# First phase of a streaming encoder step: weight tiles ahead of token rows, normalised rows in two buffers, scale and shift on ScalarE

## The chip, the core and the metric

One Trainium2 chip, one core of it. The time is device microseconds of one execution of the whole step, the median of three runs; lower is better. TensorE runs the matmuls and transposes (PE in the profile, PEld its weight loads), VectorE is DVE, ScalarE is ACT, GpSimd is POOL, and SyncE (SP) issues most of the loads. Each engine runs its own instruction list in the order in which it is written and meets the others only through semaphores.

## The reference, cut to what matters

The step is a two-layer encoder over 512 prompt tokens and 32 sample tokens, 2048 features wide. Only its beginning is touched here:

```python
xp = _layer_norm(x_prompt, ln_in_g, ln_in_b)      # (512, 2048)
xs = _layer_norm(x_sample, ln_in_g, ln_in_b)      # (32, 2048)
for l in range(DEPTH):                            # 2 layers
    fq, fk, ..., gate = _in_proj(xp, w_in[l])     # z = x @ W_in
    mk, mv = _mem_kv(mem_prompt, w_mem_kv[l])     # 256 memory tokens @ (2048, 1024)
    outs = (_fox_prompt(...), _band_prompt(...), _band_prompt(...), _cross(mq, mk, mv))
    xp = _merge(xp, outs, gate, w_out[l], ln_g[l], ln_b[l])
    ...                                           # the same for xs, with caches
def _layer_norm(x, g, b):
    mu = jnp.mean(xf, -1, keepdims=True)
    var = jnp.mean(jnp.square(xf - mu), -1, keepdims=True)
    return (xf - mu) * lax.rsqrt(var + LN_EPS) * g + b
```

## The kernel before, in words

**Split products.** A weight tile is 128 output columns of a matrix, held as `WR` [128, 2 slots, 16 chunks, 128]. Every matmul operand is split into a rounded high part and the rest: ScalarE casts `WR` to `WH` (`w_hi`, line 1012), VectorE subtracts to get `WL` (`w_lo`, line 1549), and TensorE runs three passes of 16 chunks per tile: WH by high input, WL by high input, WH by low input. The passes wait on `hi` and `lo`. A tile with 256 memory columns is 48 matmuls (`mem_tile`, line 952). Even tiles use slot 0, odd tiles slot 1; a new tile is loaded into a slot once `w_lo` of the tile two before is done (`load_first`, `load_weights`), is cast once the matmuls of that tile are done (`zd`), and can be multiplied once its result has been copied out of PSUM (`zf`, `MT` copy in `mem_done`).

**The first phase** (0 to 82.5 us) is layer 0's eight memory tiles, called tile 0 to 7 here, and beside them the first layer norm. The token rows come as five tiles of rows (`XT` four times 128 tokens, `XTS` 32 tokens; queue order in `sync`). Each gets a row sum (`first_sum`: tile 0 on ScalarE, the others on VectorE), a mean (`first_mean`), a sum of squared differences on ScalarE (`first_square`), then one shared reciprocal root (`first_rstd`, with `first_seed` on ScalarE) and the normalisation in place (`first_norm`, line 2131). TensorE transposes the rows chunk by chunk into three rotating PSUM banks (`turn_x`, line 934: four transposes per 128 features; the sample rows in one go ahead of chunk 0, line 928). VectorE applies scale and shift per feature into `OY` (`first_affine`, line 2149), ScalarE casts to `XH` (`first_hi`, line 1447) and issues the output of two chunks at a time, and VectorE subtracts to get `XL` (`x_lo`, line 2090). The sample columns have their own steps (`first_sample`, `first_sample_low`).

**What sets the order.** The lists `PE_PLAN`, `ACT_PLAN`, `DVE_PLAN` give for layer 0 the order of these steps on each engine, by name and number: ("w", 3) on VectorE is `w_lo` of tile 5, since `w_lo` of tile 0 stands before the list and ("w1", 0) is tile 1; ("mem", j) on ScalarE is `mem_done(0, j)`, the copy out of tile j and the cast of tile j + 2; ("x", g) is a pair of chunks. `TURNED` says after which third matmul of which memory tile TensorE turns which chunk. After the eight tiles TensorE runs `forget` (lines 899 and 906; the first needs all of `XH`, the second `XL` by pairs), then the first head's projections (line 579).

**Buffers.** `XT` lies over `XL`, so no part of `XL` is written until the last transpose is done: in the plan all ("low", g) stand behind ("x", 7).

Of the kernel before, what the change touches and what calls it, by code (L numbers as in the profile page):

```python
# [88 lines left out]
TURNED = {5: {2: 0, 4: 1, 7: 2, 9: 3, 12: 4, 14: 5}, 6: {2: 6, 4: 7, 7: 8, 9: 9, 12: 10, 14: 11},  # L89
          7: {1: 12, 3: 13, 5: 14, 7: 15}}  # L90
ACT_PLAN = [
    [("w1", 0), ("sum", 0), ("square", 0), ("mem", 0), ("square", 1), ("square", 2), ("mem", 1), ("square", 3),
     ("square", 4), ("seed", 0), ("mem", 2), ("mem", 3), ("mem", 4), ("sample", 0), ("x", 0), ("x", 1), ("x", 2),
     ("mem", 5), ("x", 3), ("x", 4), ("x", 5), ("mem", 6), ("x", 6), ("x", 7), ("mem", 7)],
# [3 lines left out]
    [("w1", 0), ("sum", 1), ("sum", 2), ("w", 0), ("sum", 3), ("sum", 4), ("w", 1), ("rstd", 0), ("norm", 0),  # L98
     ("w", 2), ("norm", 1), ("norm", 2), ("norm", 3), ("norm", 4), ("w", 3), ("sample", 0), ("x", 0), ("x", 1),
     ("w", 4), ("x", 2), ("mv", 4), ("x", 3), ("w", 5), ("x", 4), ("x", 5), ("mv", 5), ("x", 6), ("x", 7),   # L100
     ("low", 0), ("low", 1), ("low", 2), ("low", 3), ("low", 4), ("mv", 6), ("low", 5), ("low", 6), ("low", 7),
     ("mv", 7), ("w", 6), ("w", 7), ("tokens", 0)],
# [2438 lines left out]
```

## Time and profile before

| | us |
|---|---|
| median of 3 runs (lowest, highest) | 1881.48 (1880.87, 1881.88) |
| the profiled execution, its own time | 1881.82 |
| its span | 1879.9 |
| first head's projections start at | 82.53 |
| PE busy over the span | 1842.5 |

Start times are counted from the start of the span; the profiled execution's time is 1.9 us longer than its span. In a timeline row the first number is the start, the second the length, "x16" the instructions merged into the row, and the bracket says how long the engine stood idle just before and whose result ended that. The first phase is some 4% of the span and ends where TensorE leaves `forget`; the rest of the program isn't edited.

### The profile page before, as it was taken

Reading aid. Unit: us, or ns where it says so; the run is one execution under the profiler, and the core shown is the slowest. Engines: PE = TensorE matmul, PEld = TensorE weight load, DVE = VectorE, ACT = ScalarE, POOL = GpSimd, SP = SyncE. Lnnn points to the kernel's source line nnn. Section 1 sums busy time; section 2 is a strip of 40 time slices with the busy share of each in tenths; the row PEclk is TensorE's granted clock in tenths of the full one; section 3 lists DMA queues with packets and bytes.
Section 4 is the critical chain, followed back from the end, with each engine's and each line's share of the span. In section 5 each row is a group of like instructions: output and inputs, shape, how many; then the busy total and the mean of one; then the engine's idle time right before and its main releaser. Section 6 shows DMA issues by size and latency. Waiting matters only on the chain.

```text
span 1879.9 us, 36203 instructions
## 1 busy us (share of the span) xinstructions
PE 1842.5 (98%) x14704; PEld 1819.0 (97%) x14704; DVE 1481.5 (79%) x2085; ACT 971.9 (52%) x1583; POOL 161.3 (9%) x285
## 2 busy tenths in 40 slices
PE   7999999999999999999999999999999999999996
PEld 6999999999999999999999999999999999999996
DVE  6978877777798896777887687777788888767776
ACT  6455455444545456544574555555554555554444
POOL 0011110000000101000001111000000010100000
PEclk9999999999999999999999999999999999999998
DMA  8623333333323335655664233332333233535563
GB/s 300 235 82 125 123 125 127 115 126 105 114 104 108 112 122 186 222 205 206 217 229 152 83 123 117 119 113 99 107 110 107 96 121 106 201 137 201 198 218 133
DMA packets 71647, 273.83 MB, mean 146 GB/s; under 512 B 10136, under 2 KB 20000, under 8 KB 59184
## 3 DMA queue, kind: packets, MB, share of 16 engines
q1 hardware_dynamic: 44144, 202.12, 31.0%
q0 software_dynamic: 16928, 55.44, 8.5%
q10 hardware_dynamic: 10432, 14.29, 2.1%
q8 instruction: 98, 1.61, 0.3%
q14 instruction: 45, 0.37, 0.1%
HBM read 238.94 MB, written 35.50 MB: 146 GB/s over the span
## 4 chain that ended last, share of the span: by engine, by line
PE 87%; DVE 4%; ACT 4%; issue 2%; DMA 2%; SPq 0%; ACTq 0%; DVEq 0%
PE GB L725 46%; PE GB L637 18%; PE GB L579 8%; PE GB L952 3%; PE AB L666 3%; PE AB L708 3%; DMA WR<-in_wt 2%; PE AB L677 2%; PE GB L594 1%; ACT WH L1096 1%; ACT WH L1012 1%; DVE WL L1549 1%; DVE WL L1686 0%; PE AB L713 0%; ACT S L1026 0%
## 5 line engine op out<-in xcount | busy, mean ns | idle before, releaser
L1096 ACT CAST WH<-WR 128x1024 fp32r<-128x1024 f32 x322 | 335.9, 1048 | 403.9 <-PE GB L725 158.6
L1686 DVE TENSOR_TENSOR WL<-WR,WH 128x1024 fp32r<-128x1024 f32 x322 | 393.5, 1227 | 115.8 <-ACT WH L1096 111.6
L725 PE MATMUL GB<-XH,WH 128*128 128x272 f32 x1472 | 426.3, 290 | 2.5 <-DVE WL L1686 2.5
L725 PE MATMUL GB<-TLOW,WH 128*128 128x272 f32 x1472 | 423.8, 288 | 0.0
L725 PE MATMUL GB<-XH,WL 128*128 128x272 f32 x1472 | 423.3, 288 | 0.0
L725 PE MATMUL GB<-XL,WH 128*128 128x272 f32 x1472 | 421.1, 290 | 0.0
L725 PEld LDWEIGHTS GB<-XH,WH 128*128 128x128 f32 x1472 | 277.4, 188 | 3.4 <-DVE WL L1686 2.9
L1012 ACT CAST WH<-WR 128x2048 fp32r<-128x2048 f32 x92 | 175.6, 1908 | 198.8 <-PE GB L637 154.7
L725 PEld LDWEIGHTS GB<-XH,WL 128*128 128x128 f32 x1472 | 277.6, 189 | 0.0
L725 PEld LDWEIGHTS GB<-TLOW,WH 128*128 128x128 f32 x1472 | 276.8, 188 | 0.0
L725 PEld LDWEIGHTS GB<-XL,WH 128*128 128x128 f32 x1472 | 274.2, 188 | 0.4
L1549 DVE TENSOR_TENSOR WL<-WR,WH 128x2048 fp32r<-128x2048 f32 x92 | 210.7, 2291 | 56.6 <-ACT WH L1012 56.2
L725 PE MATMUL GB<-TX,WH 128*128 128x272 f32 x736 | 216.0, 293 | 0.0
L725 PE MATMUL GB<-TX,WL 128*128 128x272 f32 x736 | 212.3, 289 | 0.0
L637 PE MATMUL GB<-XL,WH 128*128 128x272 f32 x960 | 141.3, 288 | 0.0
L637 PE MATMUL GB<-XH,WH 128*128 128x272 f32 x960 | 140.1, 288 | 0.3 <-ACT WH L1012 0.3
L637 PE MATMUL GB<-XH,WL 128*128 128x272 f32 x960 | 140.0, 288 | 0.1
L725 PEld LDWEIGHTS GB<-TX,WH 128*128 128x128 f32 x736 | 138.4, 188 | 0.9
L725 PEld LDWEIGHTS GB<-TX,WL 128*128 128x128 f32 x736 | 138.8, 189 | 0.0
L637 PEld LDWEIGHTS GB<-XL,WH 128*128 128x128 f32 x960 | 128.4, 188 | 0.3
L637 PEld LDWEIGHTS GB<-XH,WH 128*128 128x128 f32 x960 | 127.8, 188 | 0.5 <-issue 0.5
L637 PEld LDWEIGHTS GB<-XH,WL 128*128 128x128 f32 x960 | 127.9, 188 | 0.3 <-DVE WL L1549 0.3
(281 smaller groups left out, 2906.4 us busy)
## 6 DMA issues: line engine op xcount, KB each, us to landing
WR<-in_wt SPq DMA_DIRECT2D x92, 1024.0 KB, 4.8
WR<-in_wt SPq DMA_DIRECT2D x184, 512.0 KB, 4.2
XR<-out POOLq DMA_DIRECT2D x64, 136.0 KB, 2.7
out<-OY ACTq DMA_DIRECT2D x24, 272.0 KB, 2.2
o_rest<-BD POOLq DMA_DIRECT2D x20, 272.0 KB, 5.1
out<-OY ACTq DMA_DIRECT2D x8, 544.0 KB, 6.0
out<-KT POOLq DMA_DIRECT2D x16, 272.0 KB, 2.4
out<-VT POOLq DMA_DIRECT2D x16, 272.0 KB, 2.4
```

Of the source, the lines that this page charges most:

```text
L579: mm = pe.matmul(GB[:, 2 * s + hf, 0:HALF], w[:, s, k, :], x[:, k, hf * HALF:(hf + 1) * HALF], start=(k == 0 and i == 0), stop=(k == KC - ...
L594: mm = pe.matmul(GB[:, 2 * s, 0:HALF], w[:, s, k, :], x[:, k, half(0)], start=(first and k == 0), stop=(last and k == KC - 1))
L637: mm = pe.matmul(GB[:, 2 * s + hf, 0:HALF], w[:, s, k, :], x[:, k, half(hf)], start=(at == 0), stop=(at == 3 * KC - 1))
L666: mm = pe.matmul(AB[0:r, b, at:at + w], q[:, t0:t0 + r], k, start=(p == 0), stop=(p == 2))
L677: mm = pe.transpose(AB[:, j // 4, P * (j % 4):P * (j % 4 + 1)], S[:, at:at + P], ident[:, :])
L708: mm = pe.matmul(AB[:, 3, P * i:P * (i + 1)], V[:, kb, :], pt_col(j), start=(b == 0), stop=(b == len(g.blocks[i]) - 1))
L725: mm = pe.matmul(out, w[:, k, :], x[:, k, :], start=(k == 0 and i == 0), stop=(k == KS - 1 and i == 2))
L952: mm = pe.matmul(GB[:, 2 * s, 0:NMEM], w[:, s, k, :], x[:, k, :], start=(at == 0), stop=(at == 3 * KC - 1))
L1012: act.copy(WH[:, s, :, :], WR[:, s, :, :]).then_inc(hi, 1)
L1096: act.copy(weight_block(p, name)[0], weight_source(name)).then_inc(b_hi, 1)
L1549: dve.tensor_tensor(WL[:, s, :, :], WR[:, s, :, :], WH[:, s, :, :].bitcast(F32), ALU.subtract).then_inc(lo, 1)
L1686: dve.tensor_tensor(lo_part, weight_source(name), hi_part.bitcast(F32), ALU.subtract).then_inc(b_lo, 1)
```

## The change

Six things change, all in layer 0's first phase.

1. **Load order (SP).** Weight tile 1 goes ahead of token rows 0, tile 2 (still behind `w_lo` of tile 0) ahead of rows 1, tile 3 (behind `w_lo` of tile 1) ahead of rows 3, tile 4 ahead of the three small transposition constants, and tile 5 ahead of the other constants.
2. **Row sum 2** moves from VectorE to ScalarE (`ACT_SUMS`), with a semaphore of its own, `x_sum_a`.
3. **Scale and shift** of the chunks (`first_affine`) moves to ScalarE, the cast to `XH` (`first_hi`) to VectorE. ScalarE now waits for its own result and for `x_smp` before it issues each output.
4. **Token rows** 0 and 1 lie over `TX` (`XTA`), rows 2 and 3 over the lower half of `XL` (`XTB`), so `XL`'s upper half is free from the start and ("low", 0) to ("low", 3) stand among the chunks.
5. **Transposes** are no longer in tiles 5, 6 and 7 (6, 6 and 4 chunks) but in tiles 6 and 7, eight each.
6. **In `mem_done`** of layer 0 the copy out of PSUM stands ahead of the cast of the next weight tile, and the plans of ScalarE and VectorE are written anew.

```diff
-TURNED = {5: {2: 0, 4: 1, 7: 2, 9: 3, 12: 4, 14: 5}, 6: {2: 6, 4: 7, 7: 8, 9: 9, 12: 10, 14: 11},
-          7: {1: 12, 3: 13, 5: 14, 7: 15}}
+TURNED = {6: {1: 0, 2: 1, 4: 2, 6: 3, 8: 4, 10: 5, 12: 6, 14: 7},
+          7: {0: 8, 2: 9, 4: 10, 6: 11, 8: 12, 10: 13, 12: 14, 14: 15}}
+ACT_SUMS = (0, 2)
...
-        XT = sb_at("XT", [P, NT - 1, DM], top[0])
+        XTB = sb_at("XTB", [P, 2, DM], top[0] + 4 * KS * TOK)
...
+        XTA = sb_at("XTA", [P, 2, DM], top[0])
         TX = sb("TX", [P, 2, KS, HALF], F32R)
...
+            sp.dma_start(WR[:, 1, :, :], wt[1]).then_inc(raw[1], 16)
             load_rows(0)
-            sp.dma_start(WR[:, 1, :, :], wt[1]).then_inc(raw[1], 16)
+            load_first(2)
             load_rows(1)
-            load_first(2)
             load_rows(2)
+            load_first(3)
             load_rows(3)
             load_rows(4)
+            load_first(4)
             for dst, src in ((ident, ident_d), (gT, ln_gt), (bT, ln_bt)):
                 sp.dma_start(dst[:, :], src).then_inc(s_turn, 16)
-            load_first(3)
+            load_first(5)
...
             def mem_done(l, j):
                 n, s = l * LT + j, j % 2
                 act.wait_ge(zd, n + 2)
-                w_hi(n + 2, s, l * (LT // 2) + j // 2 + 2)
+                if l:
+                    w_hi(n + 2, s, l * (LT // 2) + j // 2 + 2)
...
                 act.copy(MT[:, s, :], GB[:, 2 * s, 0:NMEM]).then_inc(zf[s], 1)
+                if l == 0:
+                    w_hi(n + 2, s, j // 2 + 2)
...
-            def first_hi(g):
+            def first_affine(g):
                 for c in range(g * GC, (g + 1) * GC):
-                    act.wait_ge(nx, c + 1)
-                    act.copy(XH[:, c, 0:SEQ], OY[:, c, 0:SEQ]).then_inc(xh, 1)
+                    act.wait_ge(x_turn, c + 2)
+                    act.activation(OY[:, c, 0:SEQ], AB[:, c % 3, :], ACT.Identity, bias=bT[:, c:c + 1],
+                                   scale=gT[:, c:c + 1]).then_inc(nx, 1)
+                act.wait_ge(x_smp, 1)
+                act.wait_ge(nx, (g + 1) * GC)
                 cs = slice(g * GC, (g + 1) * GC)
                 act.dma_start(y_o[cs].rearrange("c p t -> p c t"), OY[:, cs, :]).then_inc(o_x, 16)
...
-            def first_affine(g):
+            def first_hi(g):
                 for c in range(g * GC, (g + 1) * GC):
-                    dve.wait_ge(x_turn, c + 2)
-                    dve.tensor_scalar(OY[:, c, 0:SEQ], AB[:, c % 3, :], gT[:, c:c + 1], bT[:, c:c + 1], ALU.mult,
-                                      ALU.add).then_inc(nx, 1)
+                    dve.wait_ge(nx, c + 1)
+                    dve.tensor_copy(XH[:, c, 0:SEQ], OY[:, c, 0:SEQ]).then_inc(xh, 1)
-            def first_sample_low():
+            def first_sample_low(rows):
```

On TensorE, from tile 5 to the first chunks (`XT`, `XTA`, `XTB` are token rows, `XTS` the sample rows, `MT` a copied tile). Before:

```order
L952 MATMUL GB<-MTH,WH 128x256 [waits zf1,hi]
L952 MATMUL GB<-MTH,WH 128x256 x5
L928 MATMUL AB<-ident,XTS 128x32 [waits x_norm,s_turn]
L928 MATMUL AB<-ident,XTS 128x32 x15
L934 MATMUL AB<-ident,XT 128x128 x4
L952 MATMUL GB<-MTH,WH 128x256 x6
L934 MATMUL AB<-ident,XT 128x128 x4
L952 MATMUL GB<-MTH,WH 128x256 x4
L952 MATMUL GB<-MTH,WL 128x256 [waits lo]
```

and now:

```order
L958 MATMUL GB<-MTH,WH 128x256 [waits zf1,hi]
L958 MATMUL GB<-MTH,WH 128x256 x15
L958 MATMUL GB<-MTH,WL 128x256 [waits lo]
L958 MATMUL GB<-MTH,WL 128x256 x15
L958 MATMUL GB<-MTL,WH 128x256 x16
L924 MATMUL GB<-ident,MT 128x128 [waits s_const,zf0,tf]
L924 MATMUL GB<-ident,MT 128x128
L958 MATMUL GB<-MTH,WH 128x256 [waits zf0,hi]
L958 MATMUL GB<-MTH,WH 128x256 x2
L934 MATMUL AB<-ident,XTS 128x32 [waits x_norm,s_turn]
L934 MATMUL AB<-ident,XTS 128x32 x15
L940 MATMUL AB<-ident,XTA 128x128 x2
```

Tile 5 now runs whole, and the first transposes come three matmuls into tile 6.

On VectorE, from the reciprocal root to the chunks; the `WL` rows are tiles 4 (before only), 5 and 6. Before:

```order
L2126 SCALAR_TENSOR_TENSOR XST<-XST 128x5 [waits c_dx]
L2131 TENSOR_SCALAR XT<-XT,XST 128x2048 [waits c_dx]
L1549 TENSOR_TENSOR WL<-WR,WH 128x2048 [waits hi]
L2131 TENSOR_SCALAR XT<-XT,XST 128x2048 x3
L2131 TENSOR_SCALAR XTS<-XTS,XST 32x2048
L1549 TENSOR_TENSOR WL<-WR,WH 128x2048 [waits hi]
L2141 TENSOR_TENSOR OY<-AB,gT 128x16x32 [waits x_turn]
L2143 TENSOR_TENSOR OY<-OY,bT 128x16x32 [waits c_dx]
L2149 TENSOR_SCALAR OY<-AB,gT,bT 128x512 [waits x_turn] x4
L1549 TENSOR_TENSOR WL<-WR,WH 128x2048 [waits hi]
```

and now:

```order
L2141 SCALAR_TENSOR_TENSOR XST<-XST 128x5 [waits c_dx]
L2146 TENSOR_SCALAR XTA<-XTA,XST 128x2048 [waits c_dx]
L2146 TENSOR_SCALAR XTA<-XTA,XST 128x2048
L2146 TENSOR_SCALAR XTB<-XTB,XST 128x2048 x2
L2146 TENSOR_SCALAR XTS<-XTS,XST 32x2048
L1561 TENSOR_TENSOR WL<-WR,WH 128x2048 [waits hi]
L2156 TENSOR_TENSOR OY<-AB,gT 128x16x32 [waits x_turn]
L2158 TENSOR_TENSOR OY<-OY,bT 128x16x32 [waits c_dx]
L1561 TENSOR_TENSOR WL<-WR,WH 128x2048 [waits hi]
L2164 CAST XH<-OY 128x512 [waits nx] x6
```

Tile 4's `WL` has moved ahead of this piece; tile 5's stays behind all five normalisations and tile 6's behind the sample step.

On ScalarE, the third and fourth pair of chunks with tile 5's copy and tile 7's cast between them. Before:

```order
L1447 CAST XH<-OY 128x512 [waits nx] x2
L1449 DMA out<-OY 128x2x544
L1012 CAST WH<-WR 128x2048 [waits raw1,zd]
L1412 COPY MT<-GB 128x256 [waits o_mk1]
L1447 CAST XH<-OY 128x512 [waits nx] x2
L1449 DMA out<-OY 128x2x544
```

and now:

```order
L1456 ACTIVATE OY<-AB,bT,gT 128x512 [waits x_turn] x2
L1461 DMA out<-OY 128x2x544 [waits nx,x_smp]
L1419 COPY MT<-GB 128x256 [waits o_mk1,zd]
L1018 CAST WH<-WR 128x2048 [waits raw1]
L1456 ACTIVATE OY<-AB,bT,gT 128x512 [waits x_turn] x2
L1461 DMA out<-OY 128x2x544 [waits nx,x_smp]
```

The chunk work reads PSUM instead of SBUF, each output has a wait on the instruction just before it, and copy and cast have changed places.

## Rows read from the trace of the kernel before

**Rows 1.** Page, part 1: busy time, share of the span, instructions of each engine.

```profile
PE 1842.5 (98%) x14704; PEld 1819.0 (97%) x14704; DVE 1481.5 (79%) x2085; ACT 971.9 (52%) x1583; POOL 161.3 (9%) x285
```

**Rows 2.** Waits of TensorE from 82 us on: total us, times, longest us.

```profile
PE GB L725 <- DVE WL L1686: 2.5, 2, 1.2
```

**Rows 3.** Timeline of PE: start us, us, work [idle before <-releaser].

```profile
18.45 2.16 PE L952 MATMUL GB<-MTH,WH 128*128 128x256 f32 x16 [0.48 <-ACT WH L1012]
34.68 3.56 PE L952 MATMUL GB<-MTH,WH 128*128 128x256 f32 x16 [1.93 <-ACT MT L1412]
41.97 2.09 PE L952 MATMUL GB<-MTH,WH 128*128 128x256 f32 x16
43.97 2.17 PE L952 MATMUL GB<-MTH,WL 128*128 128x256 f32 x16
49.07 1.15 PE L928 MATMUL AB<-ident,XTS 32*128 32x32 f32 x16 [0.32 <-DVE XTS L2131]
57.80 0.38 PE L918 MATMUL GB<-ident,MT 128*128 128x128 f32 x2
74.11 4.21 PE L899 MATMUL AB<-XH,WFF 128*36 128x272 f32 x32
82.53 2.16 PE L579 MATMUL GB<-XH,WH 128*128 128x272 f32 x16
```

**Rows 4.** Windows of 1 us: busy PE, PEld, DVE, ACT, POOL; clock; DMA; GB/s.

```profile
35.00:36.00 1.00, 1.00 (x7) 1.00 (x6) 1.00 (x1) 1.00 (x1) 0.00 (x0) 0.50 0.38 131
38.00:39.00 1.00, 1.00 (x9) 1.00 (x8) 0.00 (x0) 1.00 (x2) 0.00 (x0) 0.84 0.80 246
```

**Rows 5.** Chain of waits, first 60 us: start us, us, what.

```profile
3.94 12.52 DMA WR<-in_wt
56.10 0.72 PE GB L952 x6
56.82 0.44 PE AB L934 x4
```

**Rows 6.** DMA issues between 3.3 and 3.45 us: KB, us to landing.

```profile
XT<-in_x_t SPq DMA_DIRECT2D x1, 1024.0 KB, 10.6
```

**Rows 7.** Timeline of ACT, 24 to 33 us.

```profile
24.61 0.36 ACT L1412 COPY MT<-GB 128x256 f32<-128x256 f32 x1
25.43 2.02 ACT L1428 ACTIVATE XH<-XT,XST 128x2048 fp32r<-128x2048 f32 x1 [0.46 <-ACT MT L1412]
32.37 1.90 ACT L1012 CAST WH<-WR 128x2048 fp32r<-128x2048 f32 x1 [2.84 <-DMA WR<-in_wt]
```

**Rows 8.** Timeline of DVE, 39 to 53 us.

```profile
39.07 0.17 DVE L2122 TENSOR_SCALAR XST<-XST 128x5 f32<-128x5 f32 x1 [2.48 <-ACT XH L1428]
40.37 1.35 DVE L2131 TENSOR_SCALAR XT<-XT,XST 128x2048 f32<-128x2048 f32 x1
43.83 3.85 DVE L2131 TENSOR_SCALAR XT<-XT,XST 128x2048 f32<-128x2048 f32 x3
48.85 2.27 DVE L1549 TENSOR_TENSOR WL<-WR,WH 128x2048 fp32r<-128x2048 f32 x1
51.76 0.69 DVE L2143 TENSOR_TENSOR OY<-OY,bT 128x512 f32<-128x512 f32 x1
```

**Rows 9.** Instructions of ACT by shape: busy us, mean ns | idle before.

```profile
L1389 ACT ACTIVATE OY<-OY,bT,gT 128x272 f32<-128x272 f32 x64 | 37.5, 607 | 4.0 <-ACT MT L1412 1.7 <-DVE OY L2066 1.4 <-ACT OY L1389 0.5
L1050 ACT COPY PT<-AB 128x512 f32<-128x512 f32 x32 | 17.2, 589 | 9.9 <-PE AB L677 9.9
L1043 ACT ACTIVATE S<-S,rsum 128x256 f32<-128x256 f32 x72 | 32.1, 498 | 3.8 <-DVE rsum L1601 3.7
L1043 ACT ACTIVATE S<-S,rsum 128x512 f32<-128x512 f32 x16 | 11.3, 709 | 0.0
```

**Rows 10.** Instructions of DVE by shape.

```profile
L2090 DVE TENSOR_TENSOR XL<-OY,XH 128x1024 fp32r<-128x1024 f32 x8 | 9.3, 1219 | 0.0
L1641 DVE CAST SPL<-VT 128x544 fp32r<-128x544 f32 x4 | 1.8, 445 | 0.1
```

More of the change, by code:

```diff
@@ L88 @@
      ("mv", 5), ("mem", 7), ("mv", 6), ("forget", 1)]]
-TURNED = {5: {2: 0, 4: 1, 7: 2, 9: 3, 12: 4, 14: 5}, 6: {2: 6, 4: 7, 7: 8, 9: 9, 12: 10, 14: 11},
-          7: {1: 12, 3: 13, 5: 14, 7: 15}}
+TURNED = {6: {1: 0, 2: 1, 4: 2, 6: 3, 8: 4, 10: 5, 12: 6, 14: 7},
+          7: {0: 8, 2: 9, 4: 10, 6: 11, 8: 12, 10: 13, 12: 14, 14: 15}}
+ACT_SUMS = (0, 2)
 ACT_PLAN = [
-    [("w1", 0), ("sum", 0), ("square", 0), ("mem", 0), ("square", 1), ("square", 2), ("mem", 1), ("square", 3),
-     ("square", 4), ("seed", 0), ("mem", 2), ("mem", 3), ("mem", 4), ("sample", 0), ("x", 0), ("x", 1), ("x", 2),
-     ("mem", 5), ("x", 3), ("x", 4), ("x", 5), ("mem", 6), ("x", 6), ("x", 7), ("mem", 7)],
+    [("w1", 0), ("sum", 0), ("mem", 0), ("square", 0), ("sum", 2), ("mem", 1), ("square", 1), ("square", 2),
+     ("mem", 2), ("square", 3), ("square", 4), ("seed", 0), ("mem", 3), ("mem", 4), ("x", 0), ("sample", 0), ("x", 1),
+     ("x", 2), ("mem", 5), ("x", 3), ("x", 4), ("x", 5), ("mem", 6), ("x", 6), ("x", 7), ("mem", 7)],
     [("seed", 0), ("mem", 0), ("late", 0), ("mem", 1), ("x", 0), ("mem", 2), ("x", 1), ("x", 2), ("x", 3), ("mem", 3),
@@ L97 @@
 DVE_PLAN = [
[L98 to L102, printed above, removed]
+    [("w1", 0), ("w", 0), ("sum", 1), ("mean", 2), ("w", 1), ("sum", 3), ("sum", 4), ("w", 2), ("rstd", 0),
+     ("norm", 0), ("norm", 1), ("norm", 2), ("norm", 3), ("norm", 4), ("w", 3), ("sample", 0), ("w", 4), ("x", 0),
[3 rows of a table added]
     [("rstd", 0), ("norm", 0), ("w", 0), ("norm", 1), ("late", 0), ("w", 1), ("low", 0), ("norm", 2), ("norm", 3),
@@ L319, in encoder_step @@
         x_sum = sem("x_sum")
+        x_sum_a = sem("x_sum_a")
         x_mean = sem("x_mean")
@@ L933, in turn_x @@
                 for i in range(NT - 1):
-                    mm = pe.transpose(AB[:, c % 3, P * i:P * (i + 1)], XT[:, i, P * c:P * (c + 1)], ident[:, :])
+                    mm = pe.transpose(AB[:, c % 3, P * i:P * (i + 1)], token_rows(i)[:, P * c:P * (c + 1)], ident[:, :])
                 mm.then_inc(x_turn, 1)
@@ L1471, in _ @@
                     elif kind == "x" and l == 0:
-                        first_hi(i)
+                        first_affine(i)
                     elif kind == "x":
@@ L2113, in first_mean @@
                 r = TILES[i][1]
-                dve.wait_ge(x_sum, i + 1)
+                if i in ACT_SUMS:
+                    dve.wait_ge(x_sum_a, ACT_SUMS.index(i) + 1)
+                else:
+                    dve.wait_ge(x_sum, sum(k not in ACT_SUMS for k in range(i)) + 1)
                 dve.tensor_scalar(XST[0:r, 1, i:i + 1], XST[0:r, 0, i:i + 1], -1.0 / DM, None, ALU.mult) \
@@ L2180, in _ @@
                         first_mean(i)
+                    elif kind == "mean":
+                        first_mean(i)
                     elif kind == "sample":
@@ L2183, in _ @@
                     elif kind == "x":
-                        first_affine(i)
+                        first_hi(i)
                     elif kind == "rstd" and l == 0:
@@ L2195, in _ @@
                             gate_weights_low(0)
-                            first_sample_low()
+                            first_sample_low(UPPER)
+                        if l == 0 and i == NG // 2:
+                            first_sample_low(LOWER)
                         x_lo(l, 1 if l else 0, i)
```

9 lines of the change are left out of this document (5 added, 4 removed), and 3 rows, old and new, of the table DVE_PLAN.

## The prediction

> **What bounds the kernel.** I read the page first: TensorE is busy 1842.5 of 1879.9 us [rows 1], so only what moves TensorE's path counts. The list of waits from 82 us on comes next: its longest entry is 2.5 us in all [rows 2]. From 82 us on TensorE is its own bound, and a shift of the point where it enters the first head's projections (82.53 [rows 3]) should reach the end whole. So the question is by how much that point moves. Then TensorE's timeline of the first phase: at full pace a memory tile's pass is 2.0 us (41.97 to the next at 43.97), a tile 6.0 us. Tile 0 ends at 18.45 − 0.48 = 17.97, yet tile 4 starts at 41.97 instead of 36.0: 6 us go to waits before that, 1.93 us of them ahead of tile 3, after which its first pass takes 3.56 us [rows 3]. The windows show why it is slow: the granted clock is 0.50 (1.2 GHz, against 2.4) there and back up within the window from 38 us [rows 4]. That idle costs 1.93 and then 3.56 − 2.09 = 1.5 us. From 42 us on TensorE hardly waits: tile 5, with the sample rows (1.15 us [rows 3]) and six chunks (0.44 us each, and 0.72 us for six matmuls between them [rows 5]), ends at 57.80, and the pass that needs all of XH starts at 74.11 [rows 3].
>
> **Part one: the loads.** Rows 0, fourth megabyte of the queue, land at 3.4 + 10.6 = 14.0 [rows 6]; tile 1 behind them at 3.94 + 12.52 = 16.46 [rows 5]: 2.46 us for each 1024 KB. With the queue kept full, the new order gives tile 1 at 14.0, rows 0 at 16.5, tile 2 at 18.9, rows 1 at 21.4, rows 2 at 23.9, tile 3 at 26.4 (issued at 18.2, when its slot is free), rows 3 at 28.8, the sample rows at 29.5 and tile 4 at 31.9. Tile 3 was waited for until 32.37 before [rows 7]. So tiles 1 to 4 can run at 6.0 us each without a long wait: from 17.97 to 42.0, and tile 5's first pass ends at 44.0. Taken alone that is 6.0 us ahead of before (tile 4's end 47.97), the clock loss among them.
>
> **Part two: what tile 5's second pass waits for.** It needs VectorE's subtraction of tile 5, and that stands behind all five normalisations, which need the last sum of squares on ScalarE. ScalarE's list from 16.5: row sum 0 (2.0 us, taken as a square's 2.01 [rows 7]), copy and cast of tile 2 (0.3 + 1.9) to 20.8, square 0 to 22.8, a wait for rows 2, row sum 2 from 23.9 to 25.9, copy and cast of tile 3, bound by its landing, 26.4 to 28.3, squares 1 and 2 to 32.3, copy and cast of tile 4 (2.1) to 34.4, squares 3 and 4 to 38.4, with the read-out 38.5. The output issues of the memory tiles, which before cost 0.46 us of idle each (the bracket of the square behind the first [rows 7]), now lie behind the cast and I take them at nothing: the cast covers them. If it doesn't, 0.9 us more, two issues after 26.4. VectorE began this step at 39.07 [rows 8], so the last square is 0.6 us earlier, no more: the added sum (2.0) and the added cast (1.9, with its copy) use up what the loads give. From there VectorE needs 40.37 − 39.07 = 1.3 us to the first normalisation, five of them 1.26 + 3.77 + 1.25 = 6.3, the subtraction 2.3 [rows 8]: 48.4. TensorE stands from 44.0 to 48.4, 4.4 us. Since 1.93 us was enough to halve the clock [rows 3, 4], I take another 1.5 us for it. Between 0 (the clock stays) and 2.5 (half clock for 5 us of work) this is the trace's own figure. Tile 5 ends at 48.4 + 4.0 + 1.5 = 53.9. Before it ended at 57.80 with 1.15 + 6 × 0.44 = 3.8 us of transposes in it, that is 54.0 without. **The early weights are worth nothing at this point**: 0.1 us.
>
> **Part three: tiles 6 and 7**, counted from tile 5's end. TensorE: 0.2 for turning a copied tile, three matmuls (0.35), sample rows out at 1.7. VectorE's sample step, two instructions of 0.7 [rows 8], ends at 3.1, tile 6's subtraction at 5.4. TensorE wants it at 0.2 + 2.0 + 1.15 + 3 × 0.44 = 4.7: 0.7 us idle. Chunk 3 is out at 6.1, then one each 1.16 us [rows 5]: chunk 5 at 8.4, chunk 7 at 10.7, tile 6 ends at 11.4. ScalarE's scale and shift of 512 columns from PSUM is not in the trace. Its nearest rows: 709 ns with a scale operand from memory, 589 ns for a plain copy out of PSUM, and 607 ns at 272 columns with both operands. The scale alone takes 498 at 256 and 709 at 512, so 511 at 272, and the second operand adds 0.1 [rows 9]. I take 0.80, bounds 0.59 and 0.85, 0.7 from start to start. The output issue now waits for its own engine, as the copies' issues did: 0.45 us each, eight times [rows 7]. So chunk 5 is scaled at 9.2, issue to 9.65, copy and cast of tile 7's weights to 11.75, chunks 6 and 7 to 13.25. VectorE's cast (445 ns at 544 columns) 0.4, `x_lo` 1.2 [rows 10], the subtraction 2.3: 17.15. TensorE wants it at 11.4 + 0.2 + 2.0 + 1.3 = 14.9: **2.2 us idle**. Chunk 11 is out at 17.85, chunk 15 at 22.45, tile 7 ends at 23.2, and with the next turned tile TensorE is ready at 23.4. But ScalarE, at 18.65 with chunk 11, has an issue (19.1), copy and cast (21.2), chunks 12, 13 (22.7), an issue (23.15), chunks 14, 15 (24.65), and VectorE's last cast is out at 25.1: 1.7 us idle. `forget` starts at 53.9 + 25.1 = 79.0 against 74.11: **+4.9 us**. Behind it 8.4 us as before (82.53 − 74.11): the pairs of XL come 1.2 us each, four of them already done, TensorE takes 4.1 us for the first half, so XL costs nothing. VectorE's relief (16 × 0.4 us and a sum of 2.3) hides behind waits. If the XL cover fails, 1 us.
>
> In its section "What ACT_TABLE_LOAD costs" the Trainium skill's page "ScalarE: Activation LUTs" says that an activation takes 186 ns and 0.833 ns a column, each operand from memory 93 ns more, and that neighbours overlap by 93 ns. For 512 columns with both that would be 0.80 us, 0.71 from start to start; the trace agrees at 272 columns (599 by the page, 607 measured), and by its figures the sum stays at +4.9.
>
> **Part four: the rest.** Row sum 2 saves VectorE 2.3 us ahead of a wait. The moved buffers add no wait: TX and XL's lower half are first written after the last transpose. The order of copy and cast delays a cast by 0.3 us, counted above. The sum: 1879.9 + 4.9 = 1884.8 of span, 1886.7 for the execution. That one lay 0.34 above the median, so 1886.4.
>
> **The rivals.**
> *Same waits, cheaper.* The clock does not fall (−1.5) and ScalarE's step is near its lower bound (five to eight of them count, about −0.8): +2.6, 1884. For it: the trace shows one fall of the clock, and tile 1's wait of 0.48 us left its pass at 2.16 us [rows 3]. Against: this wait is twice the one that did it.
> *Absorbed later.* VectorE is busy 79% [rows 1] and could give back the shift in the first head. Against: TensorE has no waits there to give back [rows 2]. 1881.5.
> *Heavier.* A second clock fall after the 2.2 us idle, and half clock for 5 us after the first: +0.4, +1.0, output issues in the way +0.9: 1888.7. For it: 2.2 is over 1.93.
> *Faster.* VectorE has tile 5's subtraction by 44.0 and those of tiles 6 and 7 in time, so TensorE never stands: 17.97 + 7 × 6.0 + 16 × 0.44 + 1.15 + 0.4 = 68.6 against 74.11, −5.5: 1876.0. It decides at the last square: it would have to end by 34.1 instead of 38.5. Against: ScalarE has 19 us of work and landings between 16.5 and there; rows 3 alone land at 28.8.
>
> **How the numbers follow.** Another run tells a change of 0.2% (3.8 us) from none. My case (1885 to 1888) 0.50, heavier 0.12: both slower. Cheaper, 0.22, and absorbed, 0.06, lie within 0.2%. Faster 0.10. That makes slower 0.62, within 0.28, faster 0.10. The range goes from 1880.5, below the absorbed case, to 1888.8, the heavier one; it leaves out the faster case and a little above.
>
> **What would show it.** Right: TensorE idle some 4 us ahead of tile 5's WL pass from about 44 us, released by VectorE's subtraction, the clock at 0.50 behind it; idle again for the WL passes of tiles 6 (0.7) and 7 (2.2) and before the XH pass (1.7), which starts near 79; tile 1 cast at 14.0, last square at 38.5. Wrong: `forget` starting before 76, tile 5's WL pass at 46 or earlier, or a new idle of TensorE in the heads.

## The result: 8 us slower, where 4.9 were forecast

| | before | after |
|---|---|---|
| median, us (6 runs each, same chip) | 1881.67 (1880.87 to 1883.21) | 1889.78 (1888.97 to 1891.33) |
| profiled execution, its span | 1881.82, 1879.9 | 1889.53, 1887.6 |
| tile 5's last pass ends (next work starts) | 57.80 | 57.03 |
| pass that needs all of XH starts | 74.11 | 82.94 |
| first head's projections start | 82.53 | 91.13 |

After takes 1.0045 times as long as before, 95% interval 1.0035 to 1.0055. The forecast was 1886.4 with a range to 1888.8: the direction was right, and the time lies 1.0 us above the range.

Page, part 1, of the kernel after, answering to [rows 1]:

```profile
PE 1843.5 (98%) x14704; PEld 1819.4 (96%) x14704; DVE 1472.9 (78%) x2085; ACT 976.4 (52%) x1585; POOL 160.3 (8%) x285
```

TensorE does the same work in a span 7.7 us longer. Its waits from 82 us on (total us, times, longest), answering to [rows 2]:

```profile
PE GB L731 <- DVE WL L1698: 2.5, 2, 1.2
PE AB L905 <- DVE XH L2164: 1.5, 1, 1.5
```

Only the second is new, and it is the last wait of the first phase. So the loss is made before 83 us. Timeline of PE after, answering to [rows 3] (start us, us, work [idle before <-releaser]):

```profile
44.48 2.15 PE L958 MATMUL GB<-MTH,WH 128*128 128x256 f32 x16 [0.35 <-ACT WH L1018]
51.61 3.67 PE L958 MATMUL GB<-MTH,WL 128*128 128x256 f32 x16 [4.97 <-DVE WL L1561]
62.58 0.51 PE L958 MATMUL GB<-MTH,WL 128*128 128x256 f32 x2 [0.71 <-DVE WL L1561]
74.56 0.51 PE L958 MATMUL GB<-MTH,WL 128*128 128x256 f32 x2 [1.72 <-DVE WL L1561]
82.94 4.14 PE L905 MATMUL AB<-XH,WFF 128*36 128x272 f32 x32 [1.54 <-DVE XH L2164]
```

The four waits stand where the forecast put them: 4.97 before tile 5's WL pass (forecast 4.4), 0.71 in tile 6 (0.7), 1.72 in tile 7 (2.2), 1.54 before the XH pass (1.7). The pass behind the long one takes 3.67 us instead of 2.15, and the windows show the clock (busy PE, PEld, DVE, ACT, POOL; clock; DMA; GB/s):

```profile
44.00:50.00 6.00, 2.29 (x18) 1.96 (x16) 6.00 (x6) 2.61 (x3) 0.00 (x0) 1.00 0.13 46
50.00:55.00 5.00, 3.39 (x16) 3.39 (x17) 1.55 (x1) 0.00 (x0) 0.00 (x0) 0.68 0.44 138
55.00:60.00 5.00, 5.00 (x50) 4.83 (x49) 1.06 (x2) 0.51 (x1) 0.00 (x0) 0.98 0.17 72
```

In the first of them VectorE is busy for all 6 us: it is the engine that TensorE waits for. What came out otherwise is the moment at which its chain starts. Timeline of ACT after, answering to [rows 7]:

```profile
14.05 1.91 ACT L1018 CAST WH<-WR 128x2048 fp32r<-128x2048 f32 x1
19.02 1.91 ACT L1018 CAST WH<-WR 128x2048 fp32r<-128x2048 f32 x1 [0.23 <-DMA WR<-in_wt]
24.11 1.92 ACT L1430 ACTIVATE OY<-XTB 128x2048 f32<-128x2048 f32 x1 [1.18 <-DMA XTB<-in_x_t]
28.20 1.90 ACT L1018 CAST WH<-WR 128x2048 fp32r<-128x2048 f32 x1 [1.83 <-DMA WR<-in_wt]
35.79 1.90 ACT L1018 CAST WH<-WR 128x2048 fp32r<-128x2048 f32 x1 [1.44 <-DMA WR<-in_wt]
39.59 1.99 ACT L1437 ACTIVATE XH<-XTS,XST 32x2048 fp32r<-32x2048 f32 x1
```

Tile 1 is cast at 14.05 without a wait, and tile 2 (19.02) and rows 2 (24.11) land within 0.2 us of the forecast. Tile 3 lands at 28.2 instead of 26.4, tile 4 at 35.8 instead of 31.9. ScalarE stands for both, 1.83 and 1.44 us. The forecast had it arrive just as tile 3 landed and not stand at all for tile 4. The last square ends at 41.7 instead of 38.5, 3.2 us late, and the two stands together are 3.3. Timeline of DVE after, answering to [rows 8]:

```profile
41.70 0.17 DVE L2137 TENSOR_SCALAR XST<-XST 128x5 f32<-128x5 f32 x1 [1.69 <-ACT XH L1437]
42.99 2.60 DVE L2146 TENSOR_SCALAR XTA<-XTA,XST 128x2048 f32<-128x2048 f32 x2
49.28 2.27 DVE L1561 TENSOR_TENSOR WL<-WR,WH 128x2048 fp32r<-128x2048 f32 x1
```

From 41.70 the chain takes as long as forecast: 1.3 us to the first normalisation, 6.3 for five, 2.3 for the subtraction.

### The profile page after: what moved, and what is told of

The parts are those of the page before. It is cut to its first block, busy times and chain, and to the rows that moved or that the text cites. A ratio compares the mean times of both kernels' runs of the same rounds, so it can differ in the third digit from the quotient of the medians.

```text
span 1887.6 us, 36203 instructions
## 1 busy us (share of the span) xinstructions
PE 1843.5 (98%) x14704; PEld 1819.4 (96%) x14704; DVE 1472.9 (78%) x2085; ACT 976.4 (52%) x1585; POOL 160.3 (8%) x285
## 4 chain that ended last, share of the span: by engine, by line
PE 88%; DVE 4%; ACT 4%; issue 2%; DMA 1%; ACTq 0%; DVEq 0%
PE GB L731 46%; PE GB L643 19%; PE GB L585 8%; PE AB L672 3%; PE GB L958 3%; PE AB L714 3%; PE AB L683 2%; DMA WR<-in_wt 1%; PE GB L600 1%; ACT WH L1102 1%; DVE WL L1561 1%; ACT WH L1018 1%; DVE WL L1698 0%; PE AB L719 0%; ACT S L1032 0%
```

## Experiments

Each kernel was compared with the kernel before on the same chip; behind each time stands the ratio of the two, with its 95% interval in brackets. For comparison, after stands at 1.0045. The traces are of one execution each.

**e1: the subtraction of tile 5 ahead.**

```diff
-     ("norm", 0), ("norm", 1), ("norm", 2), ("norm", 3), ("norm", 4), ("w", 3), ("sample", 0), ...
+     ("norm", 0), ("norm", 1), ("w", 3), ("norm", 2), ("norm", 3), ("norm", 4), ("sample", 0), ...
```

> The changed kernel with VectorE's subtraction of tile 5 moved between the second and third normalisation. Theory 'wait' (the forecast's): TensorE's stand of 5.0 us in tile 5 and the 1.5 us of half clock behind it are what the change costs, and both hang on the place of that one subtraction. Then WL of tile 5 is ready near 47.8 us, TensorE waits 1.3 us, the clock stays at 1.00, tile 5 ends near 51.9 instead of 57.0, forget starts near 77.8 instead of 82.9, and the time is about 5 us below the changed kernel's: 1884.7 us. Rival 'norms': the normalisations, now 2.3 us later (end 51.6), become what the transposes of tile 6 wait for, and less than 2 us is won: 1888 us or more. Rival 'chunks': the chunk steps of tiles 6 and 7 bound the phase whatever tile 5 does; forget starts at 82 or later, 1889 us.

Measured 1883.14 against 1881.23 us, 1.001 (1.0001 to 1.0019). One entry of VectorE's list, moved three places up, takes back 6.6 of the 8 us. PE timeline of e1:

```profile
47.78 2.17 PE L958 MATMUL GB<-MTH,WL 128*128 128x256 f32 x16 [1.22 <-DVE WL L1561]
57.24 0.51 PE L958 MATMUL GB<-MTH,WL 128*128 128x256 f32 x2 [0.71 <-DVE WL L1561]
69.23 0.50 PE L958 MATMUL GB<-MTH,WL 128*128 128x256 f32 x2 [1.72 <-DVE WL L1561]
77.60 4.14 PE L905 MATMUL AB<-XH,WFF 128*36 128x272 f32 x32 [1.54 <-DVE XH L2164]
```

The stand shrinks from 4.97 to 1.22 us, the pass behind it runs at 2.17 us, and the XH pass comes 5.3 us earlier. The waits of tiles 6 and 7 are unchanged to 0.01 us: they hang on tile 5's end and on nothing in front of it, as the forecast counted them. The other 1.3 of the 6.6 us lie behind the XH pass and were not traced.

**e2: only the loads.** The kernel before with the new load order in SyncE's code, all else as it was.

> The kernel before with the changed kernel's load order and nothing else. Theory 'loads are no gain by themselves': tile 3 starts near 30 us instead of 34.7 and without the half clock, but the cast of tile 4 stands behind the seed on ScalarE (last square near 39 us, cast out near 41.5), so TensorE stands 5 us before tile 4 and its clock falls there; tiles 5 to 7 and the transposes stay where they are. 1881.5 to 1883 us, no change within 0.2%. Rival 'order is the damage': the token rows land later (rows 3 near 32 instead of 28.2, sample rows 33.3 instead of 29.5), the last square moves by 3 us and everything with it: 1884.5 us or more. Rival 'order is a gain': 1878 us or less.

1881.17 against 1881.23 us, 1.0 (0.9991 to 1.0009). The earlier weights cost nothing and bring nothing, as expected, but the waits were not where I had expected them. PE timeline of e2:

```profile
28.58 3.65 PE L954 MATMUL GB<-MTH,WL 128*128 128x256 f32 x16 [2.87 <-DVE WL L1551]
38.19 3.32 PE L954 MATMUL GB<-MTH,WL 128*128 128x256 f32 x16 [2.16 <-DVE WL L1551]
75.27 4.22 PE L901 MATMUL AB<-XH,WFF 128*36 128x272 f32 x32
```

With the old lists TensorE stands for two subtractions that are queued on VectorE behind row sums (the second behind that of rows 3, which VectorE itself awaits for 2.58 us), and the clock falls twice.

**e3: rows 3 and the sample rows behind tile 4.**

```diff
             load_first(3)
+            load_first(4)
             load_rows(3)
             load_rows(4)
-            load_first(4)
```

> The changed kernel with rows 3 and the sample rows issued behind weight tile 4 instead of ahead of it. In the changed kernel tile 3's load took 4.1 us from the landing before it (24.1 to 28.2), where 2.46 was forecast. Theory 'shared': a load and the one issued right behind it share the engines, so that neither lands in turn; with nothing issued behind tile 3 until 23.3 us it lands near 26.5, its cast starts near 26.5 instead of 28.2. Rival 'slow stretch': something else slows the loads after 24 us (the output of a memory tile, small pieces); tile 3 still lands near 28. Both: tile 4 lands 3 to 4 us earlier than 35.8, rows 3 later, last square within 1.5 us of 41.7; the time within 2 us of the changed kernel's 1889.8.

1889.76 us, 1.0044 (1.003 to 1.0058). Tile 3 was cast at 27.92, which is 14.15 us behind the cast of tile 1 (13.77), the same 14.15 as in after (14.05 to 28.20). So what stands behind it in the queue does not make it late. The test is weaker than I meant it to be, since tile 4's load, issued at 23.4, took the place of what I moved. Tile 4 landed by 31 and TensorE stood shorter ahead of tile 5, but the last square (40.7) now waited for rows 3, and the XH pass starts at 82.91.

**e4: scale and shift back on VectorE, casts and outputs on ScalarE.**

```diff
-                    act.activation(OY[:, c, 0:SEQ], AB[:, c % 3, :], ACT.Identity, bias=bT[:, c:c + 1],
-                                   scale=gT[:, c:c + 1]).then_inc(nx, 1)
+                    act.copy(XH[:, c, 0:SEQ], OY[:, c, 0:SEQ]).then_inc(xh, 1)
...
-                    dve.tensor_copy(XH[:, c, 0:SEQ], OY[:, c, 0:SEQ]).then_inc(xh, 1)
+                    dve.tensor_scalar(OY[:, c, 0:SEQ], AB[:, c % 3, :], gT[:, c:c + 1], bT[:, c:c + 1], ALU.mult,
+                                      ALU.add).then_inc(nx, 1)
```

> The changed kernel with scale and shift of the chunks back on VectorE and the cast to XH with the outputs back on ScalarE; load order, row sum, buffers, places of the transposes and all other plan entries stay as changed. Theory 'wait': this exchange is no part of the loss. VectorE's steps of a chunk take 0.74 instead of 0.35 us, ScalarE's 0.55 instead of 0.70, and the outputs no longer wait; forget starts 25.9 to 26.9 us after tile 5's end as against 25.9: 1889.5 to 1890.8 us. Rival 'chunks': ScalarE's longer step and its waiting outputs are the loss in tiles 6 and 7 (2.2 + 1.7 us by the forecast); then the time is 3 to 4 us below: 1886 us.

1890.63 us, 1.0051 (1.0037 to 1.0064). The exchange is not the loss. Undone, it takes tile 7's wait from 1.72 to 0.56 us, and a turned chunk is waited for 1.36 us instead; the XH pass starts at 83.74.

**e5: TensorE kept busy while it waits.** Between the two passes of tile 5:

```diff
+                    if i == 1 and l == 0 and j == 5:
+                        for _ in range(36):
+                            pe.matmul(AB[:, 0, 0:NMEM], WH[:, s, 0, :], MTH[:, 0, :], start=True, stop=True)
                     if i == 1:
                         pe.wait_ge(lo, n + 1)
```

(The expectation calls them transposes; they are plain matmuls of tile 5's weights into a bank that is free there.)

> The changed kernel with 36 transposes of the unit matrix into a bank that nothing reads, put between the two passes of tile 5, where TensorE stands 5.0 us for VectorE's subtraction. The wait's end is not moved. Theory 'the idle engine loses its clock': the clock in 50 to 60 us stays near 1.00 instead of 0.83, the second pass of tile 5 takes 2.15 us instead of 3.67, the forget step starts at 81.4 instead of 82.94, and the kernel takes 1888.3 us, 1.5 less. Rival 'the second pass is slow because its operands or bank are contended, not by the clock': the pass still takes over 3.4 us and the time stays at 1889.8.

1887.18 against 1882.0 us, 1.0027 (1.0017 to 1.0036). PE timeline of e5, then its windows:

```profile
46.15 4.43 PE L950 MATMUL AB<-MTH,WH 128*128 128x256 f32 x36
51.27 2.17 PE L961 MATMUL GB<-MTH,WL 128*128 128x256 f32 x16 [0.69 <-DVE WL L1564]
81.07 4.13 PE L905 MATMUL AB<-XH,WFF 128*36 128x272 f32 x32 [1.55 <-DVE XH L2167]
```

```profile
50.00:55.00 5.00, 4.31 (x36) 4.11 (x36) 1.21 (x1) 0.00 (x0) 0.00 (x0) 1.00 0.50 174
```

The pass waits as long in all and then runs in 2.17 instead of 3.67 us, with the granted clock at 1.00 instead of 0.68. The slow pass is the clock, 1.5 us of it, and it falls because TensorE stood. The XH pass comes 1.9 us earlier (0.3 of that is an earlier subtraction). The medians differ by 2.6 us and the profiled spans by 0.9, so the 1.5 us are read from the pass and not from the times. Other traces show that the same stand can cost more. From the start of the WL pass to tile 5's end e1, at full clock, takes 3.9 us (47.78 to 51.69), after 5.4, e4 5.4, e10 5.8, e12 5.9, e9 6.2, e3 6.4 and e11 6.5: the low clock costs 1.5 to 2.6 us.

**e9: the outputs of memory tiles 0 and 1 late.**

```diff
-                    act.dma_start(mk_o[l, j], MT[:, s, :]).then_inc(o_mk[s], 16)
+                    if l == 0 and j < 2:
+                        act.dma_start(mk_o[l, j][0:1, :], MT[0:1, s, :]).then_inc(o_mk[s], 16)
+                    else:
+                        act.dma_start(mk_o[l, j], MT[:, s, :]).then_inc(o_mk[s], 16)
...
```

> The changed kernel, but of the outputs of memory tiles 0 and 1 only the first row goes out at its place (19 and 26 us); the other 127 rows go out four tiles later, from the buffer as it then is, so those two outputs hold the data of tiles 4 and 5. Theory 'outputs collide with the loads' (128 KB in pieces of 1 KB that land together with tile 3): tile 3 lands near 26.4 instead of 28.2, tile 4 at 33 or earlier instead of 35.8, the last square ends 1.5 to 3 us earlier than 41.7, and the kernel takes 1887 to 1888.3 us. Rival 'the loads queue behind one slow engine or one another, whatever the outputs do': tile 3 still lands at 28 or later, the last square stays within 0.5 us of 41.7 and the time at 1889.8.

(The lines that send the other 127 rows later are left out.) 1889.13 us, 1.0037 (1.0023 to 1.0051). Counted from the cast of tile 1, tile 3's cast starts 13.79 us later (13.93 to 27.72) instead of 14.15: the outputs are worth some 0.3 us of the 1.8. The last square ends 0.8 us earlier. Both fall short of what the theory asked for, and 0.3 to 0.4 of the 0.8 is spread between traces: e5 and e12, with the outputs where they were, end it that much earlier too. PE timeline of e9:

```profile
50.77 3.78 PE L959 MATMUL GB<-MTH,WL 128*128 128x256 f32 x16 [4.98 <-DVE WL L1570]
54.36 2.80 PE L959 MATMUL GB<-MTL,WH 128*128 128x256 f32 x16
```

The WL pass starts 0.84 us earlier than in after (51.61), but the two passes behind the stand take longer, and tile 5 ends at 56.99 against 57.03: the earlier square was lost again to the clock. From there to the XH pass it is 26.7 us instead of 25.9, with longer waits for ScalarE, on which the late outputs are issued. So the time of e9 says little of what earlier loads would bring.

**e10: the sample rows third in the queue.**

```diff
             load_rows(0)
+            load_rows(4)
             load_first(2)
...
             load_rows(3)
-            load_rows(4)
             load_first(4)
```

> The changed kernel with the load of the sample rows (32 partitions of 8 KB) third in the queue, behind rows 0, instead of behind rows 3. Theory 'the load of the sample rows halves the rate for about 2.5 us wherever it stands': the stretch with half the bytes per us comes near 17 to 20 us, tile 2 lands 1.5 to 3 us later than 19.0, tile 3 still lands near 28 and tile 4 is out 0 to 1 us earlier than 35.8. Rival 'the late part is the end of a long queue, whatever stands in it': bytes per us are full until 24 us, then fall near 28 us as before, tile 3 lands at 28.5 to 29. By either the last square moves by less than 1 us, since the sum of the sample rows is off the path, and the time stays within 1 us of 1889.8.

1890.91 us, 1.0048 (1.0034 to 1.0062). Windows of after, then of e10:

```profile
16.00:17.00 1.00, 1.00 (x11) 1.00 (x10) 1.00 (x1) 0.47 (x1) 0.00 (x0) 1.00 1.01 426
29.00:30.00 1.00, 0.46 (x4) 0.25 (x3) 0.00 (x0) 1.00 (x1) 0.00 (x0) 1.00 1.00 188
30.00:31.00 1.00, 0.84 (x7) 0.84 (x8) 0.86 (x1) 1.00 (x2) 0.00 (x0) 1.00 0.88 197
```

```profile
16.00:17.00 1.00, 1.00 (x11) 1.00 (x10) 1.00 (x1) 0.40 (x1) 0.00 (x0) 1.00 0.96 213
29.00:30.00 1.00, 0.19 (x2) 0.00 (x0) 0.00 (x0) 0.82 (x1) 0.00 (x0) 1.00 1.05 434
30.00:31.00 1.00, 0.00 (x0) 0.00 (x0) 0.00 (x0) 1.00 (x2) 0.00 (x0) 1.00 0.98 410
```

The stretch at half the bytes has gone from 29 to 31 us and stands at 16, with the load of the sample rows: the DMA engines are as busy as ever (0.96 of their time) and move half as much. It is shorter there than the theory had it: 15 to 18 us move 325 GB/s in the mean, which is 0.30 MB or 0.7 us short of 425, where 28 to 31 us in after, at 246, are 0.54 MB or 1.3 us short. Tile 3 is cast at 29.18, where the theory said near 28; the rival's 28.5 to 29 came nearer, though its full rate up to 24 us did not come. ScalarE does not wait for tile 4 any more; it waits 2.47 us for rows 2 instead, which now land at 26.57, and the last square still ends at 40.9.

**e11: the instruction fetch earlier.** All kernels so far have one packet on the instruction queue between 23.4 and 25.1 us. In after (DMA queues from 24 to 25 us: packets, MB, share of 16 engines):

```profile
q8 instruction: 1, 0.02, 6.8%
```

6.8% of 16 engines for 1 us is one engine for 1.1 us. Ahead of TensorE's first tile, where it waits for data anyway:

```diff
             pe.wait_ge(s_one, 1)
+            for _ in range(66):
+                pe.matmul(AB[0:32, 0, 0:32], WFF[:, 0:32], WFF[:, 0:32], start=True, stop=True)
```

> The changed kernel with 66 small matmuls of zeros on TensorE before its first tile, while it waits for the first loads; they add instructions, and nothing reads what they write. In every kernel so far one instruction fetch, a single packet of 16 KB, lies at 23.4 to 25.1 us and holds one DMA engine for 1.1 us; it follows the number of TensorE instructions, so here it should come some 8 us earlier, near 16 us, and the next near 33 instead of 41. Theory 'the fetch holds one engine, and every load has a piece on that engine': what lands from then on is 1.1 us late from 16 us on instead of from 24 us: tile 2 at 20 instead of 19.0, rows 2 at 25.2 instead of 24.1, tile 3 still at 28 to 28.5. Rival 'tile 3 is late because of what stands near it in the queue': tile 2 and rows 2 land at 19.0 and 24.1 as before and only tile 3 is late. The time: within 1.5 us of 1889.8 by both.

1889.41 against 1881.63 us, 1.0039 (1.0024 to 1.0055). The fetch came at 16.4 us, the next at 33.5. ACT timeline of e11:

```profile
14.10 1.91 ACT L1020 CAST WH<-WR 128x2048 fp32r<-128x2048 f32 x1
20.63 1.91 ACT L1020 CAST WH<-WR 128x2048 fp32r<-128x2048 f32 x1 [1.13 <-DMA WR<-in_wt]
25.75 1.92 ACT L1432 ACTIVATE OY<-XTB 128x2048 f32<-128x2048 f32 x1 [1.22 <-DMA XTB<-in_x_t]
28.36 1.91 ACT L1020 CAST WH<-WR 128x2048 fp32r<-128x2048 f32 x1 [0.35 <-DMA WR<-in_wt]
```

Tile 2 and rows 2 are now 1.6 us late, and tile 3 comes 2.6 us behind rows 2 instead of 4.1. Two traces taken for other ends agree. In e4, whose code is that of after up to the chunks, the fetch lies at 23.4 us, ahead of the landing of rows 2, and not at 24.6 as in after. ACT timeline of e4:

```profile
25.59 1.92 ACT L1430 ACTIVATE OY<-XTB 128x2048 f32<-128x2048 f32 x1 [2.71 <-DMA XTB<-in_x_t]
```

Rows 2 are 1.5 us late there (25.59 for 24.11), and tile 3 is cast at 28.14, as in after. In e10 the fetch lies at 23.9 and rows 2 come 6.37 us behind tile 2 instead of 5.09, tile 3 again 2.6 behind rows 2. So the lateness starts with the fetch, wherever it stands. The Trainium skill says why one engine is enough, in "DMA: Bandwidth & Descriptors", section "Why a DMA increments its semaphore by 16 and not by 1": a transfer is spread over up to 16 engines, and it counts as landed only when each of them has delivered its share. By that rule, as an estimate, the lag should equal the 1.1 us of the packet; measured is 1.3 (e10) to 1.6 (e11). The other 0.2 to 0.5 us stays open.

**e12: the third row sum back on VectorE.**

```diff
-ACT_SUMS = (0, 2)
+ACT_SUMS = (0,)
...
-    [("w1", 0), ("sum", 0), ("mem", 0), ("square", 0), ("sum", 2), ("mem", 1), ("square", 1), ...
+    [("w1", 0), ("sum", 0), ("mem", 0), ("square", 0), ("mem", 1), ("square", 1), ...
```

(and ("sum", 2) for ("mean", 2) in VectorE's list)

> The changed kernel with the third row sum back on VectorE (2.3 us there, between the subtractions of tiles 2 and 3). Theory 'ScalarE waits for tile 3's landing, not for its own work': ScalarE only idles 2.0 us more ahead of tile 3's cast, the cast stays at 28.2, the last square at 41.7 and the time at 1889.8, within 1 us. Rival, and the step of the forecast 'the added sum and cast use up what the loads give': without the sum the last square ends up to 2.0 us earlier and the kernel takes 1887.8 us.

1889.77 against 1881.63 us, 1.0043 (1.0028 to 1.0058). ACT timeline of e12:

```profile
28.07 1.90 ACT L1018 CAST WH<-WR 128x2048 fp32r<-128x2048 f32 x1 [3.87 <-DMA WR<-in_wt]
39.16 1.99 ACT L1437 ACTIVATE XH<-XTS,XST 32x2048 fp32r<-32x2048 f32 x1
```

ScalarE stands 3.87 instead of 1.83 us and is no earlier for it: up to tile 3's cast it waits for the transfer, not for its own work. The last square starts 0.4 us earlier than in after, but so it does in e5 (39.25), which has the sum on ScalarE.

**e7 and e8: the other waits.** e7 is e1 with VectorE's subtractions of tiles 6 and 7 and ScalarE's cast for tile 7 further ahead. e8 also puts tile 5's subtraction one place up, the next cast too, and each output issue behind the next activation:

```diff
-     ("norm", 0), ("norm", 1), ("norm", 2), ("norm", 3), ("norm", 4), ("w", 3), ("sample", 0), ("w", 4), ("x", 0),
-     ("x", 1), ("x", 2), ("low", 0), ("mv", 4), ("x", 3), ("low", 1), ("w", 5), ("low", 2), ("x", 4), ("low", 3),
+     ("norm", 0), ("w", 3), ("norm", 1), ("norm", 2), ("norm", 3), ("norm", 4), ("w", 4), ("sample", 0), ("x", 0),
+     ("x", 1), ("w", 5), ("x", 2), ("low", 0), ("mv", 4), ("x", 3), ("low", 1), ("low", 2), ("x", 4), ("low", 3),
...
-     ("mem", 2), ("square", 3), ("square", 4), ("seed", 0), ("mem", 3), ("mem", 4), ("x", 0), ("sample", 0), ("x", 1),
-     ("x", 2), ("mem", 5), ("x", 3), ("x", 4), ("x", 5), ("mem", 6), ("x", 6), ("x", 7), ("mem", 7)],
+     ("mem", 2), ("square", 3), ("square", 4), ("seed", 0), ("mem", 3), ("mem", 4), ("mem", 5), ("x", 0), ("sample", 0), ("x", 1),
+     ("x", 2), ("x", 3), ("x", 4), ("mem", 6), ("x", 5), ("x", 6), ("x", 7), ("mem", 7)],
...
+                    if c == g * GC and g:
+                        issue(g - 1)
```

> The kernel of e1 (subtraction of tile 5 behind normalisation 1) with two more moves: VectorE's subtraction of tile 6 ahead of the sample rows and that of tile 7 behind the second chunk pair, ScalarE's copy and cast for tile 7 ahead of the first chunk pair. Theory 'the waits in tiles 6 and 7 are from the same cause': of the 0.7 and 1.7 us there at least 1.8 go, the forget step starts near 75.5 instead of 77.6 and the kernel takes 1881.0 us. Rival 'they only change places': turned chunks come later by a subtraction (2.3 us), TensorE waits for those, forget stays near 77.5 and the time at 1883.

> The changed kernel with the waited-for work ahead: VectorE subtracts tile 5 behind the first normalisation, tile 6 ahead of the sample rows, tile 7 behind the second chunk pair; ScalarE copies and casts for tiles 6 and 7 earlier by a step; each output issue of a pair of chunks goes behind the first activation of the next pair. Theory 'order of the lists is what costs': tile 5's second pass starts near 46 and ends it near 50.5, tiles 6 and 7 have no wait over 0.5 us, the forget step starts at 72 to 73 against 74.1 in the kernel before, and the kernel takes 1879 to 1880 us, 1 to 2.5 less than the kernel before. Rival 'the work does not fit': the five normalisations and the chunks then come later by what the subtractions take, TensorE waits for turned chunks instead (1 to 3 us), forget starts at 75 to 77 and the time is 1882 to 1884.

e7: 1880.53 against 1881.63 us, 0.9995 (0.9986 to 1.0004); XH pass at 73.69, which is 3.9 us ahead of e1's 77.60, where some 2 us were expected. e8: 1878.56 against 1882.0 us, 0.998 (0.9971 to 0.9989), the one version here that beats the kernel before. Its PE timeline:

```profile
46.60 2.16 PE L958 MATMUL GB<-MTH,WL 128*128 128x256 f32 x16 [0.17 <-DVE WL L1567]
51.71 1.15 PE L934 MATMUL AB<-ident,XTS 32*128 32x32 f32 x16 [0.47 <-DVE XTS L2152]
71.89 4.12 PE L905 MATMUL AB<-XH,WFF 128*36 128x272 f32 x32 [0.44 <-DVE XH L2170]
```

The same operations on the same engines as in after, with the same late landings, and only the lists and the output issues in another order: no wait over 0.5 us is left behind tile 5's first pass.

## Why the forecast was right in kind and wrong in size

- **The bound and the carry.** Right within about a microsecond: a shift of the first head's start reaches the end nearly whole, 8.6 us there and 7.7 in the span. In e1 5.3 us there are 6.4 in the span. Neither difference was traced.
- **The loads, the step that failed.** "With the queue kept full", the forecast laid every load 2.46 us behind the last, by landings that all lay ahead of 24 us [rows 5, 6]. That held up to there and failed behind it: tile 3 landed at 28.2 for 26.4 and tile 4 at 35.8 for 31.9. Of tile 3's 1.8 us 1.3 to 1.6 are the lag that the instruction fetch leaves (e4, e10, e11) and some 0.3 the outputs (e9), which is about all of it. Tile 4's 3.9 are those 1.8, and 2.1 from two stretches below the full rate, in these windows of after:

```profile
24.00:28.00 4.00, 4.00 (x36) 4.00 (x35) 1.76 (x3) 2.26 (x3) 0.00 (x0) 1.00 1.01 419
28.00:32.00 4.00, 3.30 (x28) 3.10 (x27) 1.86 (x1) 3.80 (x3) 0.00 (x0) 1.00 1.04 285
32.00:36.00 4.00, 3.83 (x32) 3.63 (x31) 3.97 (x4) 2.56 (x6) 0.00 (x0) 1.00 1.01 336
```

  Against 425 GB/s the second window is 4 × 0.140 = 0.56 MB short, or 1.3 us, the third 4 × 0.089 = 0.36 MB, or 0.8 us. The shortfall of the second is gone from that place when the sample rows are moved (e10); why they cost 1.3 us here and 0.7 there stays open. What slows the third window was not tested. In it many small packets share the engines with tile 4: of the 449 from 33 to 34 us 436 are under 2 KB. They go with the three small constants, which are issued at 24 to 25 us and land 10.4 to 11.8 us later, and with the output of a memory tile. A stretch like the second was to be seen in the kernel before, where the sample rows are queued too:

```profile
26.50:29.00 2.50, 1.06 (x9) 0.85 (x8) 2.50 (x2) 2.50 (x3) 0.00 (x0) 1.00 1.05 274
```

- **The last square.** 41.7 for 38.5. The forecast said that the added sum and cast use up what the loads give. e12 shows that the sum uses up nothing, and the forecast's own list had it end at 25.9, ahead of the landing of tile 3 at 26.4; the two stands for tiles 3 and 4 (1.83 and 1.44 us) are what ScalarE lost. Up to tile 3's cast its list is bound by transfers.
- **VectorE's chain and the wait.** Right in its mechanism, and e1 shows it alone. The subtraction came 3.2 us late (51.6 for 48.4) and tile 5's first pass 2.6 (46.6 for 44.0), as the casts of tiles 3 and 4 were late: so 4.97 us for 4.4.
- **The clock.** 1.5 us forecast, 1.5 measured in after, and e5 shows the cause. That the size fits is in part luck: five other traces with a stand of 3.9 to 5.0 us at this place lost 1.9 to 2.6 us, nearer to the 2.5 that the forecast took as its upper bound.
- **Tiles 6 and 7.** From tile 5's end to the XH pass 25.9 us for 25.1. The two long waits are no longer than counted, but each ends later: counted from tile 5's end, tile 7's subtraction releases TensorE at 17.5 us for 17.15 and the last cast at 25.9 for 25.1. What ends them is ScalarE's and VectorE's chain, whose steps come late one by one (chunk 5 scaled at 9.6 for 9.2, chunk 11 at 19.3 for 18.65). TensorE also has a wait for ScalarE's cast of tile 7 that the forecast did not list:

```profile
69.42 0.44 PE L940 MATMUL AB<-ident,XTA 128*128 128x128 f32 x2 [0.38 <-ACT WH L1018]
```

  ScalarE's scale and shift took 0.78 us, inside the bounds of 0.59 and 0.85 and near the 0.80 taken. The output issues left 0.51 to 0.56 us of idle each, where 0.45 was counted.
- **Sum of the miss**, at the XH pass: 82.94 for 79.0 is 3.9 us; 3.1 of them lie ahead of tile 5's end and 0.8 behind it. That the 3.1 are the late landings is read from the chain of the trace: the stands of ScalarE, the square 3.2 us late, VectorE's steps at their forecast lengths. No run has the landings in time; what earlier loads would give with the clock as it is stays open (e9).
- **Rivals.** "Heavier" came nearest, by its size and not by its reasons: the clock did not fall a second time after 1.72 us, and the first fall cost 1.5 us and not 2.5, though in e12, e9, e3 and e11 it cost 2.0 to 2.6. "Faster" put its point of decision at the last square; e8 gets part of the gain (3.4 us in the time, where that rival had 5.5) with that square no earlier, by letting tile 5's subtraction wait for one normalisation and not for five. That the lists could be cut there was not weighed.

## What to carry to other kernels

Where a list of work alternates between two consumers, ask of each entry who stands for it: a subtraction of 2.3 us behind five normalisations of 1.3 instead of two cost 6.6 us here, and no engine was overloaded. A gain or a loss of a few tenths ahead of a point where TensorE stands long need not reach the end, since the clock behind it can take 1.5 us or 2.5. When transfers are queued back to back, do not extend the spacing of the first landings: look at the bytes moved in every window up to the last landing that you need, and at the packets of other queues in it. And when an engine's added work is charged to the path, check first that the engine is not standing for a transfer at that point anyway.
